# First expert rows by one-hot products on TensorE, and earlier requests for all parts of the expert weight ring

## The reference

```python
x = x + (merged @ w_out)
h2 = rmsnorm(x, g_norm_ffn)                       # 544 x 1024
y = hier_moe(h2, ...)
x = x + y                                         # then a final rmsnorm

def hier_moe(h, w_rg, b_rg, w_re, b_re, w_gate, w_up, w_down):
    p_top, g_top = top_k(softmax(h @ w_rg + b_rg), 1)        # 4 groups
    v_top, i_top = top_k((h @ w_re + b_re) of that group, 2) # 8 experts in a group
    gates = softmax(v_top) * p_top
    expert_id = g_top * 8 + i_top                            # 2 of 32 experts for each token
    # each expert e runs over the rows that chose it:
    out = (silu(xb @ w_gate[e]) * (xb @ w_up[e])) @ w_down[e]
    # and y sums a token's two results by its gates
```

## Time and profile before

| | us |
|---|---|
| median of 3 runs | 1082.08 |
| the runs | 1082.08, 1082.96, 1077.46 |
| the profiled execution | 1079.51 |
| its span, from first to last instruction | 1077.7 |

### The profile page before, as it was taken

How to read it: one execution, slowest core, us unless ns; L and a number is a source line. 1 busy time by engine, 2 the same in 40 slices (tenths; PEclk the granted TensorE clock), 3 DMA queues, 4 the chain that set the end, 5 groups by cost and what they waited for, 6 DMA issues and landing times.

```text
span 1077.7 us, 15220 instructions
## 1 busy us (share of the span) xinstructions
PE 981.8 (91%) x6267; PEld 682.0 (63%) x6267; DVE 383.3 (36%) x752; ACT 286.1 (27%) x492; POOL 210.0 (19%) x121
## 2 busy tenths in 40 slices
PE   9999999999999999999999999888788778987885
PEld 6986888889989999999995333333333333333332
DVE  7244834434787443312435122111111111111118
ACT  5435535544576621222204000000000000000012
POOL 0321222222312253433310011110110111011000
PEclk9999999999999999999999999999998999888898
DMA  9342432122121333433658999999999999999994
GB/s 222 95 92 78 132 94 60 42 77 69 51 60 30 101 87 88 157 94 98 243 241 331 411 428 426 423 426 429 427 428 426 428 428 427 426 428 428 423 415 162
DMA packets 108943, 267.56 MB, mean 248 GB/s; under 512 B 21821, under 2 KB 88797, under 8 KB 95666
## 3 DMA queue, kind: packets, MB, share of 16 engines
q1 hardware_dynamic: 104178, 258.06, 62.5%
q0 software_dynamic: 4704, 8.64, 2.1%
HBM read 256.12 MB, written 18.17 MB: 255 GB/s over the span
## 4 chain that ended last, share of the span: by engine, by line
PE 61%; DMA 26%; DVE 6%; ACT 3%; issue 3%; POOL 1%; SPq 0%; DVEq 0%; ACTq 0%; POOLq 0%
PE proj L1075 34%; DMA we<-in_w_exp_up 21%; PE proj L1533 12%; DMA we<-in_w_exp_down 4%; PE proj L1549 4%; PE bank L1210 2%; PE bank L1237 1%; PE bank L1223 1%; PE bank L1429 1%; DVE xsT L2586 1%; PE bank L1559 1%; PE proj L1187 1%; ACT ex L1890 1%; DVE x_rows L2666 0%; DVE hT_f L2127 0%
## 5 line engine op out<-in xcount | busy, mean ns | idle before, releaser
L1533 PE MATMUL proj<-we,xsT 128*64 128x512 f32 x512 | 249.4, 644 | 67.5 <-DMA we<-in_w_exp_up 59.8
L1535 PE MATMUL proj<-we,xsT 128*64 128x512 f32 x512 | 249.8, 645 | 0.0
L938 POOL TENSOR_TENSOR wlo<-raw,whi 128x1024 fp32r<-128x1024 f32 x68 | 156.6, 2304 | 384.5 <-PE proj L1075 360.6
L1533 PEld LDWEIGHTS proj<-we,xsT 128*64 128x64 f32 x512 | 72.9, 148 | 210.0 <-issue 198.9
L1075 PE MATMUL proj<-hT_hi,whi 128*128 128x272 f32 x688 | 147.0, 295 | 2.5 <-POOL wlo L938 1.4
L1075 PE MATMUL proj<-hT_hi,wlo 128*128 128x272 f32 x688 | 145.2, 293 | 0.0
L1075 PE MATMUL proj<-hT_lo,whi 128*128 128x272 f32 x688 | 145.0, 292 | 0.0
L2578 DVE TENSOR_TENSOR hg<-hg,proj 64x512 f32<-64x512 f32 x32 | 22.1, 690 | 307.1 <-ACT hg L2046 293.0
L2046 ACT ACTIVATE hg<-proj 64x512 f32<-64x512 f32 x30 | 17.7, 590 | 421.2 <-PE proj L1535 421.2
L1549 PE MATMUL proj<-we,hT 128*64 128x512 f32 x256 | 115.2, 593 | 1.8 <-DVE hT L2581 1.1
L1550 PE MATMUL proj<-we,hT 128*64 128x512 f32 x256 | 115.2, 593 | 0.0
(11 more groups left out here) (374 smaller groups left out, 1388.8 us busy)
## 6 DMA issues: line engine op xcount, KB each, us to landing
we<-in_w_exp_gate SPq DMA_DIRECT2D x31, 2048.0 KB, 32.6
we<-in_w_exp_up SPq DMA_DIRECT2D x31, 2048.0 KB, 36.9
we<-in_w_exp_down SPq DMA_DIRECT2D x31, 2048.0 KB, 39.3
raw<-in_w_in SPq DMA_DIRECT2D x43, 512.0 KB, 3.8
x_rows<-in_x_prompt SPq DMA_DIRECT2D x8, 512.0 KB, 4.8
raw<-in_w_branch_b SPq DMA_DIRECT2D x8, 512.0 KB, 4.2
raw<-in_w_out SPq DMA_DIRECT2D x8, 512.0 KB, 4.1
zc<-expert_out SPq DMA_DIRECT2D x4, 1024.0 KB, 17.8
```

The lines of the kernel that those rows point to most:

```text
L938: nc.gpsimd.tensor_tensor(lo[:, 0:c], raw[n % NRAW][:, 0:c], hi[:, 0:c].bitcast(F32), ALU.subtract).then_inc(w_split, 1)
L1533: pe.matmul(proj[0:SLOTS, s, 0, :], xsT[:, k, cols], wg[:, k * FF:(k + 1) * FF], start=(k == 0), stop=(k == KD - 1))
L1535: mm = pe.matmul(proj[64:64 + SLOTS, s, 0, :], xsT[:, k, cols], wu[:, k * FF:(k + 1) * FF], start=(k == 0), stop=(k == KD - 1))
```

## The change

It has four parts.

1. The rows of experts 0 and 1 aren't gathered. `first_at` (DVE) gives each token its lane in expert 0 or 1, `first_pick` is its one-hot form over 2 x 64 lanes, and PE multiplies the normalised rows by it: for each of 8 slices and 5 row tiles one 128x128 float32 product. The result is what `turn_rows` made before. The gather and its eight transposes go.
2. `h2` goes. `normed_row` writes the scaled rows into `X` itself, from which SP stores `rows` and PE reads; after the stores and the products ACT multiplies them back by the root (`plain_row`), one tile after the silu of each of the first five experts. The areas of routing maps move to other places in SBUF.
3. (2, 2) is asked for together with (2, 0), and (2, 1) together with (1, 2). Expert 3's gate and up parts are asked for in halves, the first halves when PE has done four of the eight steps of up(0).
4. On PE, `x2_rows(4)` comes before the ranks, `WARM` falls from 4 to 1 and both `unread(2)` go. The maps of second choices and of the last experts' gates (`late_maps`) move behind up(0), and DVE's work on them (`late_numbers`) behind the first `gated`.

```diff
-WARM = 4
+WARM = 1
...
         load_expert(2, 0, 2)
+        load_expert(2, 2, 2)
         for i in range(NT):
             sp.wait_ge(h2_ready, i + 1)
-            sp.dma_start(rows[i * P:i * P + ROWS[i], :], h2[0:ROWS[i], i, :]).then_inc(rows_stored, 16)
+            sp.dma_start(rows[i * P:i * P + ROWS[i], :], X[0:ROWS[i], i, :]).then_inc(rows_stored, 16)
         sp.wait_ge(x2_turned, 7 + NT)
         load_expert(1, 2, 1)
-
-        sp.wait_ge(xs_loaded, 16)
         load_expert(2, 1, 2)
-        load_expert(2, 2, 2)
...
+        sp.wait_ge(first_half, 1)
+        for part in range(2):
+            load_expert(0, part, NSETS, slice(0, 2048), half_loaded[part])
         sp.wait_ge(up_done, 1)
         for part in range(2):
-            load_expert(0, part, NSETS)
+            load_expert(0, part, NSETS, slice(2048, 4096))
...
-        gather(xsb, P, xs_loaded)
-        pool.wait_ge(ys_zeroed, 16 * NZERO)
...
+        pe.wait_ge(h2_ready, NT)
+        pe.wait_ge(onehots_ready, 1)
+        for k in range(KD):
+            for i in range(NT):
+                r = ROWS[i]
+                mm = pe.matmul(bank[:, k // 4, (k % 4) * P:(k % 4 + 1) * P], X[0:r, i, :].rearrange("r (p k) -> r k p", k=KD)[:, k, :],
+                               first_pick[0:r, i, :, :].rearrange("r e l -> r (e l)"), start=(i == 0), stop=(i == NT - 1))
+        mm.then_inc(xsT_done, 1)
...
+                if first:
+                    late_maps()
...
-        unread(2)
-        turn_rows(16)
...
-            nc.scalar.mul(h2[0:r, i, :].rearrange("p (a b) -> p a b", a=2), x2_source(i)[0:r], st_x[0:r, 4, i:i + 1])\
+            nc.scalar.mul(X[0:r, i, :].rearrange("p (a b) -> p a b", a=2), x2_source(i)[0:r], st_x[0:r, 4, i:i + 1])\
...
-            nc.scalar.copy(X[0:r, i, :].rearrange("p (a b) -> p a b", a=2), x2_source(i)[0:r]).then_inc(x2_copied, 1)
+            nc.scalar.mul(X[0:r, i, :], X[0:r, i, :], st_x[0:r, 1, i:i + 1]).then_inc(x2_copied, 1)
...
+        run(v.scalar_tensor_tensor(first_at[:, :, :], rank[:, :, 0:2], 1.0, picks[:, :, 0:2], ALU.add, ALU.mult))
+        run(v.tensor_scalar(first_at[:, :, :], first_at[:, :, :], -1.0, 1.0, ALU.mult, ALU.add))
+        v.tensor_tensor(first_pick[:, :, :, :], first_at[:, :, :].unsqueeze(3).to_broadcast([P, NT, 2, SLOTS]),
+                        con("neg_lane").unsqueeze(1).unsqueeze(1).to_broadcast([P, NT, 2, SLOTS]), ALU.is_equal).then_inc(onehots_ready, 1)
```

More of the change, by code:

```diff
@@ L350, in _build @@
     g_fin = R("g_fin", [P, D])
+    W_RT = R.at
     w_rt = R("w_rt", [P, KD, 64])
@@ L1536, in up @@
                                start=(k == 0), stop=(k == KD - 1))
+                if half_done and k == KD // 2 - 1:
+                    mm.then_inc(half_done, 1)
             mm.then_inc(done, 1)
@@ L1575, in pair @@
                     pe.wait_ge(we_loaded[u % NSETS][part], it * 32 + 16 * (u // NSETS) + 16)
-                up(s, slice(s * SLOTS, (s + 1) * SLOTS), w[0], w[1], up_done)
+                    if isinstance(it, int) and it == 0 and u == NSETS:
+                        pe.wait_ge(half_loaded[part], 16)
+                first = s == 0 and first_pair(it, m)
+                up(s, slice(s * SLOTS, (s + 1) * SLOTS), w[0], w[1], up_done, half_done=first_half if first else None)
+                if first:
+                    late_maps()
                 if u or not first_pair(it, m):
@@ L2531, in _, with turned_rows @@
                 .then_inc(onehots_ready, 1)
+        def turned_rows(done):
+            for b in range(2):
+                last = v.tensor_tensor(xsT[:, 4 * b:4 * b + 4, :], bank[:, b, :].rearrange("p (k l) -> p k l", k=4),
+                                       g_rows[:, 4 * b:4 * b + 4].unsqueeze(2).to_broadcast([P, 4, P]), ALU.mult)
+            last.then_inc(done, 1)
+        dve.wait_ge(xsT_done, 1)
+        turned_rows(xsT_copied)
         dve.wait_ge(maps_done, 1)
         token, choice = bank[:, 2, 0:NBLK], bank[:, 3, 0:NBLK]
-        for s in range(2):
-            lane = slice(s * SLOTS, (s + 1) * SLOTS)
-            last = v.tensor_scalar(gidx[lane, :], token[lane, s:s + 1], float(VACANT), None, ALU.add)
-        last.then_inc(gidx_ready, 1)
         run(v.tensor_scalar(G1[:, :], token, float(VACANT), None, ALU.add))
@@ L2565, in _, with late_numbers @@
         run(v.tensor_scalar(S1[:, :], G1[:, :], 4.0, con("half"), ALU.mult, ALU.add))
[L2566 to L2574 removed]
+        def late_numbers():
+            dve.wait_ge(second_done, 1)
+            dve.wait_ge(gate_rows_done, 1)
+            run(v.scalar_tensor_tensor(S1[:, :], choice, 2.0, S1[:, :], ALU.mult, ALU.add))
+            dve.wait_ge(meta_ready, 1)
+            dve.wait_ge(late_loaded, 32)
+            v.tensor_copy(last_slots[:, :], bank[:, 3, NBLK:NBLK + 2])
+            for s in range(2):
+                last = v.tensor_scalar(pick[s][:, :], numbers, G1[:, NE - 2 + s:NE - 1 + s], None, ALU.is_equal)
+            last.then_inc(picks_ready, 1)
         def gated(s, done):
@@ L2581, in hidden_copy @@
             v.tensor_copy(hT2[:, s, :, :], bank[:, 2 + s, 0:4 * SLOTS].rearrange("p (k l) -> p k l", k=4)).then_inc(done, 1)
-        def turned_rows(done):
-            for b in range(2):
-                last = v.tensor_tensor(xsT[:, 4 * b:4 * b + 4, :], bank[:, b, :].rearrange("p (k l) -> p k l", k=4),
-                                       g_rows[:, 4 * b:4 * b + 4].unsqueeze(2).to_broadcast([P, 4, P]), ALU.mult)
-            last.then_inc(done, 1)
         def rows_out(it, u):
```

87 lines of the change are left out of this document (37 added, 50 removed).

## The result

The changed kernel took **1094.23 us** (median of 4 runs, 1092.81 to 1094.90) against 1081.98 for the kernel before (4 runs, 1077.46 to 1082.96). The ratio is 1.0116, with a 95% interval of 1.0097 to 1.0134: slower by 1.2%, clear of the scatter, where no measurable change was forecast, and 9.7 us above the range's upper end.

What follows compares the result with a forecast made beforehand. Expert bytes bound the end from about 588 us, released by request R. Up(0) 2.3 us earlier, less 0.8 lost to late maps, moves R by -1.5 us: 1080.6 us against 1082.08, range 1075.6 to 1084.5.

Steps and rivals of the forecast that it cites:

- 80 x 0.111 = 8.9: One-hot products on PE: 80 records at the transposes' spacing of 0.111 us take 8.9 us, over at 583.3.
- seam's first request: Request for part (2, 0) at 562.81; the seam is 564 to 588 us, where DMA moves only 307 GB/s.
- to up(0): Behind the products, DVE scales and PE makes 40 small map products; up(0) starts at 585.1, 2.3 us earlier.
- up(0) to its request: From up(0)'s start to the request for expert 3's two parts: 7.13 us.
- that request to R: After up(0)'s request: late maps lose 0.8 us, and up(1) keeps its clock fall and 1.84 us extra length.
- R: Request for expert 4's two parts behind up(1), at 605.55; it moves by -1.5 us and the end with it.
- A dip before R: DMA stream: the seam's gap closes and reopens from 599, some 5 us close to 0 before expert 4's parts.
- the rows are stored by 579: Row stores on SP: finished by 579 although (2, 2) goes ahead of them, so the remaining gather is covered.
- The clock stays up: Rival: late maps keep PE occupied, no clock fall after up(0), up(1) gains 1.84 us more: 1078.8; chance 0.22.
- The fall comes in the products: Rival: the clock falls in the one-hot products, costs 1.84 us, R moves by +0.3: 1082.4; chance 0.16.
- The gap is won whole: Rival: transfers don't wait for R, all bytes the windows lack come back, 8.2 us: 1073.9; chance 0.10.
- Slower: the products run at 1.2 GHz: Rival: one-hot products take 17.8 instead of 8.9 us, R comes 7.4 us later than before: 1089.5; chance 0.08.

Runs made afterwards that it cites:

- e1_contiguous: Changed kernel, but the one-hot products read 128 adjacent values of a row instead of every eighth: 1080.13 us, ratio 1.0003.
- e11_before_halves: Kernel before, with gate and up parts of experts 3 and 4 asked for in halves, first ones halfway through up(0) and up(1): 1080.39 us, ratio 0.9991.
- e7_wide: Changed kernel, but the one-hot tile is the weight, 512 adjacent columns are streamed in 20 records, and picked rows are copied and transposed: 1080.88 us, ratio 0.9990.
- e3_gather: Changed kernel with the one-hot products undone: experts 0 and 1 gathered and transposed again, the rest kept: 1089.96 us, ratio 1.0082.
- e4_before_delay: Kernel before, with 17 more unread products of 128x512 on PE ahead of up(0): 1095.89 us, ratio 1.0143.
- e2_step4: Changed kernel, but the one-hot products read every fourth value (16 bytes) instead of every eighth: 1092.05 us.
- e5_swapped: Changed kernel with the one-hot products' operands swapped, the one-hot tile as weight and the rows with their 32-byte step streamed: 1094.1 us.
- e2_step2: Changed kernel, but the one-hot products read every second value (8 bytes) instead of every eighth: 1078.71 us.
- e9_filler: Changed kernel with one unread dense product of 512 columns ahead of each of the eight slices of one-hot products: 1098.12 us.

## Why the prediction was wrong, step by step

The forecast was 1080.6 us and the measured median is 1094.23, 13.6 above. In the profiled executions they are 16.9 apart, 1076.2 (1077.7 - 1.5) and 1093.1 in the span: the one of before lay 2.6 under its median, the one of after 0.7 above. The range's ends, 1075.6 and 1084.5, come out of its own terms as 1075.7 and 1084.4, which changes nothing.

**The step that failed: "so 80 x 0.111 = 8.9".** The price of a record was taken from the transposes, since "they load as large a weight tile and stream 128 columns each". Same shape, other instruction: a product costs 0.15 us with adjacent operands, and 0.253 to 0.275 at the full clock with the 32-byte step that the diff plainly shows. The prediction says nothing of the step. Its price is that of transposes of adjacent values (those of `yT` at 572.32 in the earlier trace rows). The transposes of `xsb` in the same rows read with the step of 32 bytes and are as fast (1.05 us for eight), so no row of transposes could warn of it: it was the wrong operation to be near to. The upper bound, 17.8 us, doubled the transposes for the clock and had no room for the step either; with 23.67 the truth lay outside both bounds. The term is off by 14.7 us of the 16.9.

**The rest of the sum, term by term.**

| term | forecast | after | difference |
|---|---|---|---|
| seam's first request | 562.81 | 564.16 | +1.35 |
| from there to the products' start | 11.5 | 11.39 | -0.1 |
| the products | 8.9 | 23.6 | +14.7 |
| to up(0) | 1.9 | 2.81 | +0.9 |
| up(0) to its request | 7.13 | 8.89 | +1.8 |
| that request to R | 11.8 | 10.03 | -1.8 |
| R to the end | 472.15 | 472.2 | +0.05 |

The differences add up to 16.9. The 1.35 us at the seam belong to no part of the change: kernels with the same code up to there have it anywhere between 561.95 and 565.25. The maps and the first steps of up(0) are longer because the products leave the clock at 0.50 (the 40 records of the maps 2.88 instead of 1.77 us in e1_contiguous, and four steps of 0.85 us instead of 0.43).

**What held.** R sets the end: 472.15 us behind it before and 472.2 after, with 15 us more in front. For a later R that is one to one; for an earlier one it takes a closed gap as well (e11_before_halves). A dip before R was forecast, and there is one, 66 GB/s from 620 to 622; but the main one, from 594 to 607.41, stands ahead of expert 3's first halves, which were to come in time. In e7_wide, where they do, the dip is where it was put. `first_pick` was ready 1.1 us after the forecast 574.3, and by 1.35 us the seam itself was later. ACT's plain rows and DVE's late numbers hide behind PE. That the rows are stored by 579 was wrong, without effect here: the last store goes out at 575.1 and lands 9.2 us later, but the gather that is left goes out at 603.70; in e3_gather the same delay is part of the loss. And the sum without the wrong term comes out near the measurement, in part by luck: e7_wide, whose products take 9.40 us, has 1080.88 us, and the forecast was 1080.6; but its R - seam is 43.21, where the forecast had 42.74 - 1.5 = 41.2.

**The rivals.** *The clock stays up* was right for up(1) in the changed kernel and in e1_contiguous: from up(0)'s request to R 10.03 and 10.04 us, where 11.8 - 1.84 = 10.0 was its sum. In e7_wide it fell as the forecast had it (11.74 us). The prediction took the fall in up(1) as a fixed part of the kernel before, but of three kernels with the same PE stream there only one has it (11.03 us; e4_before_delay has 9.34 and e11_before_halves 9.19). These runs don't show what decides between the two. *The fall comes in the products* came true, and cost 1.7 to 3.4 us in the products and 2.9 behind them, not 1.84. *The gap is won whole* is refuted by e1_contiguous: its window from 576 to 586 has 403 GB/s, its dip from 604 to 607 has 74, and the time is that of before. *Slower: the products run at 1.2 GHz* had the right place, the right sign and the right rule from product time to R; only its 17.8 us lacked the step. Its threshold held: 12.05 us (e1_contiguous) are not measurable, 23.67 are. It had a chance of 0.08 because the clock was taken for the only thing that could make the products slow. A product of a kind that no row shows deserved a wider upper bound, and this rival a larger share.

On the gather, the Trainium skill's rule (GPSIMD Engine Reference, sections 4.1 and 8: the only option for indirect DMAs) was weighed against one-hot products. The runs say that products can take the gather's place at no loss when they read adjacent columns (e7_wide, 0.9990), and lose 1.2% when they don't.

## What to carry to other kernels

Price a new instruction by a row with the same operation and the same access pattern, and where none exists, say so and leave the upper end open: the step between the elements that PE reads changed the price of a float32 product by a factor of 1.7 to 1.9 at the full clock, and transposes of the same shape and step did not show it. When a stream of weights is bound by a ring, find the first request that the compute side releases; a delay ahead of it reaches the end whole. A gap closed ahead of it and the request made earlier each gave nothing alone here; together they gave 0.3%. Don't take a fall of the clock seen in one execution as a fixed term. Ask for bulk data early only if nothing that the compute side is about to wait for has to pass it, and count the stores that such a load waits for.

## What was not expected of the hardware

- A float32 product of 128 weights x 128 columns, two records, takes 0.15 us a record at a granted clock of 1.00 with operands of a 4-byte step, 0.157 with 8 bytes, and 0.253 to 0.275 with 32. With 16 bytes it costs as much as with 32: 2.69 and 2.75 us for the first ten records, still at 1.00. It makes little difference which operand has the step (23.67 and 22.79 us).
- Transposes that read with the 32-byte step aren't slowed: 8 in 1.05 us in the kernel before and 8 in 1.16 in e7_wide, against 1.04 for 8 with adjacent values.
- The granted clock fell to 0.50 while PE was busy all the time, in each of the three kernels whose strided products ran back to back (after, e2_step4, e5_swapped), and stayed there for 27 us in the first; it did not fall in the products of e1_contiguous, e2_step2, e7_wide, and not with dense products between the slow ones (e9_filler). The Trainium skill (TensorE: Matmul & The Clock Gate, What's actually happening) has activity release the clock from its throttle; a PE row that says busy is no sign of it in this trace, 2.00 of 2.00 us busy at 0.50.
- At half the clock the strided record takes 0.30 us instead of 0.275 (70 records in the 20.9 us from 578.30 on), far from double, while the maps' 40 records take 2.88 instead of 1.77.
- A gather from GpSimd's queue that had to pass some parts asked for earlier kept PE waiting 13.30 us, and 6.04 with two parts fewer. Of the difference 1.6 us are the row stores' later landing (8.4 to 9.1 us after their issue instead of 2.5 to 3) and 5.6 the gather's own way.
